# Row sums of the exponentials in a dilated attention: from ScalarE's accumulators to VectorE reductions two steps behind

## The reference, cut to what matters

```
logits = jnp.einsum('brnqhd,brnkhd->brnhqk', qs, kb) + bias[None, None, None]
logits = jnp.where(valid[None, None, :, None], logits, -jnp.inf)
m = jnp.max(logits, axis=-1, keepdims=True)
p = jnp.exp(logits - m)
l = jnp.sum(p, axis=-1, keepdims=True)
o = jnp.einsum('brnhqk,brnkhd->brnqhd', p / l, vb)
lse = (m + jnp.log(l))[..., 0]
...
wts = jax.nn.softmax(jnp.stack(lses), axis=0)
o = jnp.sum(wts[..., None] * jnp.stack(outs), axis=0)
```

## Time and profile before

| | us |
|---|---|
| median of 3 runs | 3014.29 (3012.89 to 3014.92) |
| the profiled execution: its own time | 3014.49 |
| its span in the trace | 3012.7 |
| TensorE, matmuls busy | 2897.0 (96%) |
| TensorE, weight loads busy | 2486.5 (83%) |
| VectorE busy | 1436.4 (48%) |
| ScalarE busy | 1120.9 (37%) |
| GpSimd busy | 119.8 (4%) |

### The profile page before, as it was taken

One profiled execution on the slowest core, in us unless ns is written; L12 is line 12 of the kernel. 1 busy time (PEld: TensorE's weight loads), 2 busy tenths in 40 slices (PEclk: granted clock), 3 DMA queues, 4 the chain that ended last, 5 costly groups with the idle time before them and its releaser, 6 DMA issues. The chain is left out here.

```text
span 3012.7 us, 39596 instructions
## 1 busy us (share of the span) xinstructions
PE 2897.0 (96%) x16452; PEld 2486.5 (83%) x16452; DVE 1436.4 (48%) x1613; ACT 1120.9 (37%) x1551; POOL 119.8 (4%) x116
## 2 busy tenths in 40 slices
PE   8989999999999899999999988999999999899999
PEld 8889999998987588888777787788887887778887
DVE  5664333233513634444477745544455865643322
ACT  5444332132232324332255534343224446544321
POOL 0000000001400000000000010000001310000000
PEclk9999999999999999999999999999999999999999
DMA  4212332322222135556432220355563431033332
GB/s 130 68 40 74 89 92 77 96 94 91 70 84 70 29 94 147 165 154 179 123 101 79 75 43 29 112 158 156 163 184 102 112 98 32 21 91 97 93 87 85
DMA packets 409379, 292.70 MB, mean 97 GB/s; under 512 B 24851, under 2 KB 388180, under 8 KB 409250
## 3 DMA queue, kind: packets, MB, share of 16 engines
q1 hardware_dynamic: 403210, 286.68, 32.6%
q0 software_dynamic: 1600, 3.55, 0.7%
q10 hardware_dynamic: 4440, 0.64, 0.2%
HBM read 286.16 MB, written 4.13 MB: 96 GB/s over the span
## 5 line engine op out<-in xcount | busy, mean ns | idle before, releaser
L201 DVE TENSOR_TENSOR w_lo<-w_raw,w_hi 128x2048 fp32r<-128x2048 f32 (+3 forms) x237 | 497.8, 2101 | 525.0 <-ACT w_hi L195 524.5
L195 ACT ACTIVATE w_hi<-w_raw 128x2048 fp32r<-128x2048 f32 (+3 forms) x237 | 416.3, 1757 | 258.2 <-PE ps L282 150.4
L280 PE MATMUL ps<-ffn_h_hi,w_hi 128*128 128x264 f32 (+1 forms) x1008 | 323.5, 321 | 2.4 <-DVE w_lo L201 2.4
L282 PE MATMUL ps<-ffn_h_hi,w_lo 128*128 128x264 f32 (+1 forms) x1008 | 322.7, 320 | 0.0
L281 PE MATMUL ps<-ffn_h_lo,w_hi 128*128 128x264 f32 (+1 forms) x1008 | 321.4, 319 | 0.0
L280 PE MATMUL ps<-up_act_hi,w_hi 128*128 128x512 f32 (+1 forms) x880 | 308.2, 350 | 0.0
L282 PE MATMUL ps<-up_act_hi,w_lo 128*128 128x512 f32 (+1 forms) x880 | 307.3, 349 | 0.0
L281 PE MATMUL ps<-up_act_lo,w_hi 128*128 128x512 f32 (+1 forms) x880 | 305.7, 347 | 0.0
L280 PE MATMUL ps<-up_h_hi,w_hi 128*128 128x512 f32 x672 | 265.3, 395 | 6.4 <-DVE w_lo L201 6.4
L282 PE MATMUL ps<-up_h_hi,w_lo 128*128 128x512 f32 x672 | 265.3, 395 | 0.0
L281 PE MATMUL ps<-up_h_lo,w_hi 128*128 128x512 f32 x672 | 262.8, 391 | 0.0
(11 more groups left out here) (580 smaller groups left out, 5633.5 us busy)
## 6 DMA issues: line engine op xcount, KB each, us to landing
mod_raw<-in_w_ada_dram SPq DMA_DIRECT2D x128, 384.0 KB, 3.9
w_raw<-in_ffn_w_gu_dram SPq DMA_DIRECT2D x88, 512.0 KB, 5.3
w_raw<-in_w_ffn_in_dram SPq DMA_DIRECT2D x88, 512.0 KB, 5.3
w_raw<-in_ret_w_in_dram SPq DMA_DIRECT2D x24, 1024.0 KB, 5.1
w_raw<-in_ffn_w_down_dram SPq DMA_DIRECT2D x32, 704.0 KB, 5.0
w_raw<-in_w_ffn_out_dram SPq DMA_DIRECT2D x32, 704.0 KB, 4.7
w_raw<-in_dsw_w_in_dram SPq DMA_DIRECT2D x18, 1024.0 KB, 5.0
w_raw<-in_gdn_w_in_dram SPq DMA_DIRECT2D x16, 1024.0 KB, 5.6
```

Of the source, the lines that this page charges most:

```text
L195: self.nc.scalar.activation(self.w_hi[:, s, 0:w.size], self.raw[:, s, 0:w.size], ACT.Copy).then_inc(self.hi_ready, 1)
L201: self.nc.vector.tensor_tensor(self.w_lo[:, s, 0:w.size], self.raw[:, s, 0:w.size], self.w_hi[:, s, 0:w.size].bitcast(F32), ALU.subtract). ...
L280: nc.tensor.matmul(out, w_hi, h_hi, start=first, stop=False)
L282: return nc.tensor.matmul(out, w_lo, h_hi, start=False, stop=last)
```

## The change

ScalarE's exponentials lose their `accum_out`. A new VectorE function `row_sums(n)` reduces the exponentials of step n with one `tensor_reduce` over the keys, and signals a new semaphore `summed`. It is called after step n + 2, and for the last two steps after step 23. VectorE's step n now also waits for `summed` of step n - 3, and `mask` waits for `summed` where it waited for `exp`. TensorE, SyncE and GpSimd are given the same instructions as before.

```
@@ __init__
-                  ("loaded", "scores", "taken", "max", "exp", "masked", "turned", ...
+                  ("loaded", "scores", "taken", "max", "exp", "summed", "masked", "turned", ...
@@ scalar: exps
                 ins = nc.scalar.activation(self.s[:, n % 3, u, 0:nk], self.s[:, n % 3, u, 0:nk], ACT.Exp,
-                                           bias=self.minus[:, n % 3, head[u]:head[u] + 1],
-                                           accum_out=self.sums[:, quad, g, b, head[u]:head[u] + 1])
+                                           bias=self.minus[:, n % 3, head[u]:head[u] + 1])
@@ vector: step
             if n >= 3:
                 dve.wait_ge(S["turned"], n - 2)
+                dve.wait_ge(S["summed"], n - 2)
@@ vector
+        def row_sums(n):
+            quad, g, b = self.steps[n]
+            dve.wait_ge(S["exp"], n + 1)
+            nc.vector.tensor_reduce(self.sums[:, quad, g, b, :].rearrange("p (c two) -> p two c", two=2),
+                                    self.s[:, n % 3, :, 0:P * len(self.tiles(n))].rearrange("p (two c) k -> p two c k", two=2),
+                                    AX_X, ALU.add).then_inc(S["summed"], 1)
+
         def mask(quad, g):
-            dve.wait_ge(S["exp"], self.last(quad, g) + 1)
+            dve.wait_ge(S["summed"], self.last(quad, g) + 1)
@@ vector: the loop over the items, after a step and ahead of weights and mask
+            if what >= 2:
+                row_sums(what - 2)
+            if what == 2 * per - 1:
+                row_sums(what - 1)
+                row_sums(what)
             if what == per + 3:
                 weights(0)
```

More of the change, by code:

```diff
@@ L3448, in __init__ @@
         self.S = {n: K.sem("dilated_" + n) for n in
-                  ("loaded", "scores", "taken", "max", "exp", "masked", "turned", "copied", "out", "kept", "shifted",
+                  ("loaded", "scores", "taken", "max", "exp", "summed", "masked", "turned", "copied", "out", "kept", "shifted",
                    "e", "w", "weights_0", "weights_1", "weights_2", "mixed", "hi", "lo")}
```

## The result

| | before | after |
|---|---|---|
| median, us (14 runs each, lowest to highest) | 3013.08 (3011.73 to 3020.97) | 3021.64 (3015.05 to 3027.18) |
| the profiled execution: its own time, us | 3014.49 | 3018.05 |
| its span in the trace, us | 3012.7 | 3016.3 |
| first addition of the stage to the output projection, us | 91.63 | 100.52 |

The ratio is 1.0023, 95% interval 1.0015 to 1.0031: slower by 6.9 us, 4.5 to 9.3; the two medians alone are 8.6 us apart. The median of after lies in the forecast range, but 1.1 us above the likeliest case (3017.5 to 3020.5) and at the top end of the rival with the lower clock (3020.8 to 3021.6). The interval straddles the 0.2% bound, so the data don't decide between "no change" and "slower" as the chances had them.

What follows compares the result with a forecast made beforehand. It took TensorE to set the pace in one-tile steps and VectorE around the first mixing; 1.79 + 1.48 + 1.14 + 0.61 + 0.15 + 0.0 = +5.2 us gave 3019.5 us, range 3015.0 to 3022.5.

Steps and rivals of the forecast that it cites:

- the likeliest case: Whole kernel: row sums on VectorE's path add 5.2 us, time 3019.5 us, clock effect taken as 0; chance 0.50.
- the rival with the lower clock: First mix product and turn(11): TensorE's longer idle wait brings the low clock, +1.3 us, up to +2.1; chance 0.30.
- start to step 13: VectorE from step 3 to step 13: runs without rest with row sums added, so step 13 starts 1.07 us later.
- step 14 to spread (0,0): VectorE to step 16: row sums 12 and 13 come in, 0.27 us of waiting goes, +1.48 us.
- spread (0,1) to (0,2): Row sum 16 stands between step 18 and VectorE's part of spread (0,1), delaying spread (0,2) by 0.61 us.
- the four places named: First mixing: TensorE waits for VectorE before the mix product 1.42 us and spreads (0,0) 1.74, (0,1) 0.58, (0,2) 0.60.
- the distance is that of maximum to negation, 0.72 us: VectorE's queue: price of a 512-column row sum when the next instruction waits for it, 0.72 us.
- the thin cover in one-tile steps: Steps after step 4: VectorE's 2.25 us a step stays under TensorE's 2.41, leaving 0.16 us.
- the tightest place for TensorE on the way: Before step 13: step 4's addition, done at 2522.39, just before the scores of step 6 at 2522.46.
- Hidden row sums: Whole stage: row sums fall into VectorE's idle time, leaving 3014.3 us, give or take 1; chance 0.13.
- ScalarE as the bound: One-tile steps: ScalarE's 2.50 us period sets the pace, so 96 x 0.09 comes off, 3005.7 us; chance 0.05.
- Tail: Before the last mask: ScalarE saves 0.7 us, the last row sum adds 0.72, so 0.0 us.

Runs made afterwards that it cites:

- e5: The changed kernel with idle products on TensorE inside its gaps before the first mix product and the first half's three spreads; 1.0013 of the kernel before.
- e8: The kernel before, accumulators untouched, with idle products filling TensorE's gaps at the first mixing and in the tail; 0.9979 of the kernel before.
- e1: The kernel before without ScalarE's accumulators and with no row sums in their place, the sums filled once with ones; 0.9997 of the kernel before.
- e3: VectorE sums only steps 4 to 9 and 18 to 22, the other 13 keep ScalarE's accumulators; 0.9999 of the kernel before.
- e10: The changed kernel with VectorE's wait for the row sum written first of a step's three waits, not last; one run, 3014.05 beside 3014.14.
- e2: The changed kernel with ScalarE's accumulators kept as well, into a tile nobody reads; 1.0018 of the kernel before.
- e9: All 24 row sums on VectorE inside the steps, with idle products in TensorE's gaps in both halves; 1.0003 of the kernel before.
- e7: The changed kernel with each row sum moved to between a step's addition and its maxima; 1.0012 of the kernel before.
- e4: The changed kernel with idle products on TensorE placed behind the wait for scores taken, in the path and not the gap; 1.0047 of the kernel before.

## Why the prediction was right, and where it was off

The sum's terms against the marks, each as what is added between two marks: once after less before, and once e5 less e8, the same two kernels with the clock held up to the last mask (their tails are filled differently, so the way to the projection can't be compared):

| term | forecast | measured | clock held |
|---|---|---|---|
| start to step 13 | 1.07 | 1.94 | 1.93 |
| mask waits for row sum 11 | 0.72 | 0.73 | 0.72 |
| mix product and turn(11): the clock | 0 (rival 1.3) | 1.25 | -0.01 |
| step 14 to spread (0,0) | 1.48 | 2.05 | 1.42 |
| spread (0,0) to (0,1) | 1.14 | 0.77 | 1.10 |
| spread (0,1) to (0,2) | 0.61 | 2.20 | 0.57 |
| to the scores of step 21 | 0.15 | 0.19 | 0.19 |
| to the last mask | 0.0 | -0.06 | -0.04 |
| to the projection | 0 | -0.18 | |
| sum | 5.2 | 8.9 | 5.9 |

**Right: the mechanism.** ScalarE didn't set the pace (e1, 0.9997), VectorE's reductions are on the path from the start to step 13 and at the four places named, TensorE's waits, and free where TensorE set the pace (e3). With the clock held on both sides (e5 against e8), the last mask comes 81.89 - 76.01 = 5.9 us later, against 5.2 summed, in VectorE's timelines, first e5, then e8 (whose first additions stand at 2510.30 and 2509.47):

```profile
2592.19 0.22 DVE L3699 TENSOR_TENSOR dsw_masked<-dsw_tops,dsw_blocks 128x64 f32<-128x64 f32 x1
...
2585.48 0.22 DVE L3700 TENSOR_TENSOR dsw_masked<-dsw_tops,dsw_blocks 128x64 f32<-128x64 f32 x1 [4.11 <-ACT dsw_s L3613]
```

There every term but the first is within 0.06 us of its forecast.

**Luck: how near the time came.** Both errors named next point to slower, and the clock's share of the lengthening, 3.0 us, is over half of the sum. The width of the range took them in; the likeliest case did not.

**Mis-sized: "the distance is that of maximum to negation, 0.72 us".** It was 0.81. Ten chained row sums stand before step 13, and 10 x 0.09 = 0.9 is about the 0.87 that this term missed. The forecast had an upper end of 0.03 us for each added wait; it was 0.09 to 0.10, and e10 shows that it depends on the wait's place among three, and the records show the wait instruction that takes the time. So the thin cover in one-tile steps, 0.16 us, was 0.07 (2.41 - 2.34). Also missed: the tightest place for TensorE on the way. It was not step 4's addition but step 3's, for which the scores of step 5 waited 0.49 us; VectorE's delay swallowed that.

**Taken at 0 and not 0: the clock.** The rival put a drop at the mix for 1.3 us; the profiled run shows it with 1.25, and three more entries that I hadn't placed, each as measured less forecast: 0.52 of step 14 to spread (0,0) (step 15 waited for turn(12), which ran at the lower clock), 1.63 in spread (0,1), and -0.37 around spread (0,0). That is 3.0 us together, about as much as e5 takes back in the first half: its spread (0,2) is 68.09 - 63.31 = 4.8 us earlier, of which 1.6 are the low stretch at spread (0,0) that the kernel before has too, so 3.2. The forecast and its slower rival were drawn as alternatives; in this run both came, on top of each other. e2, with the same work on VectorE, shows the same drops. Whether they fall so in every execution of the changed kernel is not shown; the time's interval, 4.5 to 9.3 us, takes in both this trace's 8.9 and the 5.9 without them.

**The other rivals.** Hidden row sums: with the clock held, 5.9 us stay (e5 against e8), and some 3.7 with the sums inside the steps (e9). ScalarE as the bound: e1. The rule that speaks for it (the Trainium skill, Perfetto Trace Analysis, "Identifying the Most-Contended Engine": judge TensorE by its useful arithmetic against the peak and by its weight loads, not by matmul time) was used here by the weight loads alone, and so used it is not borne out in this stretch: weight loads at 13.30 of 17.00, and yet TensorE's period stayed at 2.40 us with ScalarE relieved. The other rule weighed (the Trainium skill, VectorE: DVE Perf Modes, "The DRAIN you can't avoid") was given in the prediction without its exception, in the same section: "A next op that is not held starts earlier". This case's traces agree with the exception: e7's 0.59 us behind an instruction of 0.68, where nothing is waited for.

**Tail.** Relief there was worth 1.05 us (e2), not 0.7; the last row sum took 0.72 of it back, and in all the way from the scores of step 21 to the last mask came out at -0.06 us, 0.0 forecast. What took the other 0.3 is open.

## What to carry to other kernels

Look where the receiving engine is idle before moving work to it, not how much: VectorE had 30.7 us to spare in the stage and 19.4 of work still cost 5.9, because in the first steps and in the mixing it had none, and e3 shows such work free elsewhere. Price an instruction by the distance to what stands behind it in its queue, waits included, not by its length. And a longer wait of TensorE can cost twice, once as the wait and once in the clock behind it; filling the gaps with idle products gave 0.2% on the kernel as it was (e8), as long as they stood in the gap and not behind it (e4).

## What the runs showed of the hardware that was not expected

- An addition with three waits started 0.81 us behind the row sum that it waited for when that wait was written last, and 0.71 us behind it when it was written first (1.35 and 1.25 for 1024 columns). Written last, it stood in a wait instruction of its own between the two; written first, it was carried by the addition, and the wait instruction stood ahead of the row sum. The kernel before, with two waits an addition, has such an instruction too, with one wait and 0.02 us long; what a fourth wait costs was not tried.
- TensorE kept the full clock through idle products that nobody reads: with 3.19 us of them in a gap of 4.0 the granted clock stayed at 1.00 and the mix product took 1.07 us, without them it fell to 0.54 and the product took 1.94.
- The length of a wait alone didn't decide on the clock: ahead of spread (0,0), 1.74 us of waiting came with a product of 2.80 us before, 1.75 with one of 2.05 in e10. What else decides was not tested.
- Layers upstream that no edit touched differ by up to 6 us between profiles (first addition at 2505.05 to 2510.92). Where that comes from is open. For an edit worth 5 us in one stage, the marks inside the trace decide more than the total.
